# First input-projection unit by token blocks, next six units as three rounded products

## The reference

```
proj = h @ w_in                       # (256, 1024) @ (1024, 3328)
q_a, k_a, v_a, q_h, i_h, zf_fwd, zf_bwd, z_g = split(proj)
mix = concat(attention(q_a, k_a, v_a), recurrence(q_h, i_h, zf_fwd, zf_bwd, z_g)) @ w_out
h = layer_norm(alpha * h + mix)
for e in range(32): out += gate[:, e] * (swiglu(h @ w_up[e] + b_up[e]) @ w_down[e] + b_down[e])
h = layer_norm(alpha * h + out)
```

## Time and profile before

| | us |
|---|---|
| median of 3 runs | 1110.83 |
| the profiled execution, device time | 1110.73 |
| its span in the trace | 1109.0 |
| PE busy | 1043.1 (94% of the span) |
| DVE busy | 236.9 (21%) |
| ACT busy | 174.2 (16%) |
| HBM traffic | 428.31 MB, 386 GB/s mean |
| line L1040, records of 256 columns x272 | 62.0 busy, 391 ns for one |

### The profile page before, as it was taken

The page is one execution under the profiler, slowest core; times in us unless marked ns, Lnnn a source line. Parts: engine busy times, 40 slices in busy tenths (PEclk is TensorE's granted clock), DMA queues, the critical chain, the costliest instruction groups (busy, mean ns, idle before and its releaser), DMA issues.

```text
span 1109.0 us, 12478 instructions
## 1 busy us (share of the span) xinstructions
PE 1043.1 (94%) x5087; PEld 446.1 (40%) x5087; DVE 236.9 (21%) x650; ACT 174.2 (16%) x353; POOL 23.7 (2%) x31
## 2 busy tenths in 40 slices
PE   7999999999999999999999999999999999999995
PEld 6888656333333333333333333333333333333333
DVE  5186344111111111111111111111111111110114
ACT  2173211111111111111111111111111111110111
POOL 2500000000000000000000000000000000000000
PEclk8999999999999999999999999999999999999998
DMA  9733797999999999999999999999999999999993
GB/s 322 210 101 76 286 367 312 390 419 430 428 427 427 428 428 427 427 430 427 428 427 428 428 427 427 429 426 428 428 427 428 428 426 429 426 428 428 428 427 136
DMA packets 45934, 428.31 MB, mean 386 GB/s; under 512 B 4992, under 2 KB 18336, under 8 KB 21216
## 3 DMA queue, kind: packets, MB, share of 16 engines
q1 hardware_dynamic: 44352, 427.18, 92.9%
q10 hardware_dynamic: 1536, 0.43, 0.2%
HBM read 426.02 MB, written 1.05 MB: 385 GB/s over the span
## 4 chain that ended last, share of the span: by engine, by line
PE 67%; DMA 23%; DVE 7%; issue 2%; ACT 0%; DVEq 0%; ACTq 0%
PE bank L1291 27%; PE bank L1347 16%; DMA ring<-in_w_up_dram 15%; PE bank L1040 8%; PE bank L1246 4%; DMA lncat<-in_w_up_dram 4%; DMA mixa<-in_w_up_dram 4%; PE bank L1071 3%; DVE wbuf L971 2%; PE bank L1332 2%; DVE wbuf L966 2%; PE bank L1254 2%; DVE wbuf L975 1%; DVE wbuf L965 1%; PE bank L1302 1%
## 5 line engine op out<-in xcount | busy, mean ns | idle before, releaser
L1291 PE MATMUL bank<-ring,wbuf 128*64 128x512 f32 x1280 | 285.4, 593 | 9.4 <-DMA ring<-in_w_up_dram 9.4
L1291 PEld LDWEIGHTS bank<-ring,wbuf 128*64 128x64 f32 x1280 | 90.4, 137 | 187.3 <-issue 162.0
L1347 PE MATMUL bank<-ring,wbuf 128*64 128x512 f32 x640 | 145.0, 595 | 0.0
L594 ACT ACTIVATE wbuf<-wbuf 128x256 f32<-128x256 f32 x64 | 26.6, 416 | 480.3 <-DVE wbuf L965 480.3
L956 DVE TENSOR_SCALAR hT<-iota_s,hT 128x64 f32<-128x64 f32 x62 | 12.9, 251 | 409.1 <-PE bank L1291 409.1
L965 DVE TENSOR_SCALAR wbuf<-bank 128x256 f32<-128x256 f32 x64 | 26.9, 420 | 338.2 <-PE bank L1291 338.2
L1291 PE MATMUL bank<-wbuf 128*64 128x512 f32 x384 | 88.7, 593 | 0.4 <-DMA wbuf<-in_w_up_dram 0.4
L1347 PEld LDWEIGHTS bank<-ring,wbuf 128*64 128x64 f32 x640 | 44.6, 137 | 82.0 <-issue 79.6
L1261 PE MATMUL bank<-wbuf,putT 64*128 64x512 f32 x264 | 65.6, 615 | 0.7 <-ACT wbuf L604 0.7
L1040 PE MATMUL bank<-hT,wbuf 128*128 128x256 f32 x272 | 62.0, 391 | 2.4 <-ACT hT L464 2.4
L1246 PE MATMUL bank<-X,hT 128*64 128x512 f32 x256 | 62.0, 605 | 0.1
(11 more groups left out here) (240 smaller groups left out, 740.7 us busy)
## 6 DMA issues: line engine op xcount, KB each, us to landing
ring<-in_w_up_dram SPq DMA_DIRECT2D x80, 2048.0 KB, 31.4
ring<-in_w_down_dram SPq DMA_DIRECT2D x40, 2048.0 KB, 31.2
wbuf<-in_w_up_dram SPq DMA_DIRECT2D x24, 2048.0 KB, 31.1
mixa<-in_w_up_dram SPq DMA_DIRECT2D x12, 2048.0 KB, 32.9
lncat<-in_w_up_dram SPq DMA_DIRECT2D x12, 2048.0 KB, 32.2
wbuf<-in_w_down_dram SPq DMA_DIRECT2D x12, 2048.0 KB, 33.0
wbuf<-in_w_in_dram SPq DMA_DIRECT2D x13, 1024.0 KB, 9.8
mixa<-in_w_down_dram SPq DMA_DIRECT2D x6, 2048.0 KB, 33.2
```

What stands on the lines that cost most here:

```text
L594: a.activation(sig[:, w], glu[:, w], ACT.Sigmoid, scale=SIG_ALPHA).then_inc(s["sig_ready"], 1)
L1291: ins = mm(bank[n][c * SLOTS:(c + 1) * SLOTS, :], xT[:, k, :], wk[:, o:o + 512], start=(k == 0), stop=(k == KT - 1))
L1347: ins = mm(bank[2][c * SLOTS:(c + 1) * SLOTS, :], actT[:, at:at + SLOTS], wk[:, a * D + c * 512:a * D + (c + 1) * 512], start=(i == 0 and ...
```

## The change

Two things are changed in the input projection.

Unit 0 is worked by token blocks: for each token tile its 16 matmuls have 128 moving columns in place of 256, and each waits only for the parts of `hT` that it reads. The small transpose of `rows` is moved ahead of the first hT step on PE, and the copies of `embT` and `lbt` on DVE are moved to stand between the two token tiles.

Units 1 to 6 are each computed as three products of rounded operands. ACT writes a copy of the unit in float32r (`w_high`, 128 x 2048) and of hT (`h_high`, two copies of 128 x 1024). DVE subtracts them from the originals to get the low parts (`w_low`, written over the unit itself, and `h_low`). PE then adds up w_high x h_high, w_low x h_high and w_high x h_low, each over all eight k, in place of one float32 product. The high parts of the units go round four slots of `ring` (halves 6 to 9), `h_high` and `h_low` are in halves 10 and 11. The product w_low x h_low is left out.

The copies and subtractions are put between the other work of ACT and DVE as the diff shows: ACT makes the high parts of units 1 to 4 before the Exp table, its four DMA issues and `lb_exp`, and those of 5 and 6 after the copies of qa. DVE makes the low parts of units 1 and 2 and of hT before the small tensors, 3 after the wait for `lb_exp`, 4 after the work on X, and 5 and 6 between the copies of kv and `gates`.

```diff
@@ -4,6 +4,7 @@
 from concourse import mybir
 
 F32 = mybir.dt.float32
+F32R = mybir.dt.float32r
 BF16 = mybir.dt.bfloat16
 I32 = mybir.dt.int32
 U32 = mybir.dt.uint32
@@ -70,6 +71,7 @@
     UNITS = [(n, h) for n, _, w in GROUPS for h in range(w // 256)]
     UI = {u: i for i, u in enumerate(UNITS)}
     WBUF = 6
+    SPLIT = range(1, 7)
 
     with ExitStack() as ctx:
         def sb(name, shape, dt=F32):
@@ -82,6 +84,9 @@
 
 
 
+        with nc.sbuf_tensor("ring_r", [P, CHUNKS, CW], F32R) as ring_r, \
+                nc.sbuf_tensor("wbuf_r", [P, WBUF // 2, 4096], F32R) as wbuf_r:
+            pass
         ring = sb("ring", [P, CHUNKS, CW])
         halves = ring[:, :, :].rearrange("p c (a n) -> p (c a) n", a=2)
         wbuf = sb("wbuf", [P, WBUF // 2, 4096])
@@ -132,6 +137,15 @@
 
         def w_raw(u):
             return wbuf[:, u % WBUF // 2, u % 2 * 2048:(u % 2 + 1) * 2048]
+
+        halves_r = ring_r[:, :, :].rearrange("p c (a n) -> p (c a) n", a=2)
+        h_high, h_low = (halves_r[:, i, :].rearrange("p (k n) -> p k n", k=KT) for i in (10, 11))
+
+        def w_high(u):
+            return halves_r[:, 6 + (u - SPLIT[0]) % 4, :]
+
+        def w_low(u):
+            return wbuf_r[:, u % WBUF // 2, u % 2 * 2048:(u % 2 + 1) * 2048]
 
         lncat = sb("lncat", [P, 2 * TT * D])
         lnp = lncat[:, 0:2 * D].rearrange("p (i n) -> p i n", i=2)
@@ -205,7 +219,7 @@
         names = ("x_in0 x_in1 emb_in rows_in ln1_in ln2_in par_in "
                  "wout_in bias_in braw_in bup_split bup_in zeroed consts h_ready lb_ps proj_done job_done logf_ready logf_in exps_in "
                  "k_ready var_ready std_ready zg_sig mx_ready prob_ready prob_shared rec_cat rms_std mix_half "
-                 "mix_done hT_params x1_ready logit_done top_ready g4_ready mask_ready gate_ready "
+                 "mix_done hT_params h_high_ready h_low_ready w_high_ready w_low_ready x1_ready logit_done top_ready g4_ready mask_ready gate_ready "
                  "rank_done ex_ready route_done key_ready sel_ready plan_ps plan_ready lbm_ready lb_exp "
                  "kpT_ready aT_ready S_ready chunk_used picked put_ps gath_done xg_ready xT_ps actT_ps "
                  "scat_done plan_read put_ready xT_ready actT_ready y_ready glu_ready sig_ready act_ready "
@@ -468,6 +482,21 @@
                     if k == 2:
                         settle()
                 read(ins, ("hT", t, 0))
+
+            def high(u):
+
+                act.wait_ge(win_in[u % WBUF], 16 * (u // WBUF + 1))
+                if u - 4 in SPLIT:
+                    act.wait_ge(s["proj_done"], u - 4 + 1)
+                a.copy(w_high(u), w_raw(u)).then_inc(s["w_high_ready"], 1)
+
+            high(1)
+            for i in range(2):
+                for t in range(TT):
+                    job_is_read(act, ("hT", t, i))
+                a.copy(h_high[:, 4 * i:4 * i + 4, :], hT[:, 4 * i:4 * i + 4, :]).then_inc(s["h_high_ready"], 1)
+            for u in SPLIT[1:4]:
+                high(u)
             preload(ACT.Exp)
             act.dma_start(sink[:, :], attn_sink[0].partition_broadcast(P)).then_inc(s["par_in"], 16)
             act.dma_start(normg[:, :], hgrn_norm_g[0].partition_broadcast(P)).then_inc(s["par_in"], 16)
@@ -531,6 +560,8 @@
             q4 = qaT.rearrange("p j n -> p (j n)")
             tick(a.copy(tiles_of(q4, 0), pair("qa", 0)))
             a.copy(tiles_of(q4, 1), pair("qa", 1)).then_inc(proj_read[GI["qa"]], 1)
+            for u in SPLIT[4:]:
+                high(u)
             sig_gate(0)
             log_gate(0)
             probs(0)
@@ -642,9 +673,10 @@
                 link(v.reciprocal(rstd[:, t:t + 1], rstd[:, t:t + 1]))
                 v.tensor_scalar(X[:, t, :], X[:, t, :], mv[:, t, 0:1], rstd[:, t:t + 1], ALU.subtract,
                                 ALU.mult).then_inc(s["h_ready"], 1)
-            dve.wait_ge(s["lb_ps"], 1)
-            v.tensor_copy(embT[:, :, :], bank[7][:, 16:32].rearrange("p (m k) -> p m k", m=2)).then_inc(s["hT_params"], 1)
-            tick(v.tensor_copy(lbt[:, :, :, :], bank[7][:, 0:16].rearrange("p (d i h) -> p d i h", d=2, i=2)))
+                if t == 0:
+                    dve.wait_ge(s["lb_ps"], 1)
+                    v.tensor_copy(embT[:, :, :], bank[7][:, 16:32].rearrange("p (m k) -> p m k", m=2)).then_inc(s["hT_params"], 1)
+                    tick(v.tensor_copy(lbt[:, :, :, :], bank[7][:, 0:16].rearrange("p (d i h) -> p d i h", d=2, i=2)))
             dve.wait_ge(s["hT_params"], 1)
             for t in range(TT):
                 job_is_done(dve, ("hT", t, 1))
@@ -657,6 +689,20 @@
                         settle()
                 read(ins, ("hT", t, 1))
 
+            def low(u):
+
+                dve.wait_ge(s["w_high_ready"], u - SPLIT[0] + 1)
+                v.tensor_tensor(w_low(u), w_raw(u), w_high(u).bitcast(F32), ALU.subtract).then_inc(s["w_low_ready"], 1)
+
+            low(1)
+            for i in range(2):
+                dve.wait_ge(s["h_high_ready"], i + 1)
+                for t in range(TT):
+                    job_is_read(dve, ("hT", t, i))
+                k4 = slice(4 * i, 4 * i + 4)
+                v.tensor_tensor(h_low[:, k4, :], hT[:, k4, :], h_high[:, k4, :].bitcast(F32),
+                                ALU.subtract).then_inc(s["h_low_ready"], 1)
+            low(2)
             link(v.tensor_tensor(lbs[:, :, :], lbt[:, :, 0, :], lbt[:, :, 1, :], ALU.max))
             v.tensor_tensor(lbe[:, :, :, :], lbt[:, :, :, :],
                             lbs[:, :, :].unsqueeze(2).broadcast_to([P, 2, 2, NH]), ALU.subtract).then_inc(s["lbm_ready"], 1)
@@ -672,11 +718,13 @@
             link(v.tensor_tensor(lb[:, :, :], lbe[:, :, 0, :], lbs[:, :, :], ALU.mult))
             link(v.tensor_scalar(oml[:, :, :], lb[:, :, :], -1.0, 1.0, ALU.mult, ALU.add))
 
+            low(3)
             job_is_done(dve, ("hT", 1, 1))
             dve.wait_ge(s["emb_in"], 32)
             for t in range(TT):
                 link(v.tensor_tensor(X[:, t, :], X[:, t, :], lnp[:, 0, :], ALU.mult))
                 link(v.tensor_tensor(X[:, t, :], X[:, t, :], lnp[:, 1, :], ALU.add))
+            low(4)
             unit_is_done(dve, "kv")
             for g in range(NG):
                 for o in range(2):
@@ -684,6 +732,8 @@
             tick(v.tensor_copy(va[:, :, :], proj_bank("kv", 1)[:, 0:TOK].rearrange("p (t n) -> p t n", t=TT)))
             settle()
             dve.sem_inc(proj_read[GI["kv"]], 1)
+            low(5)
+            low(6)
 
             def cseq(ap):
                 return ap.rearrange("p (c n) -> p c n", n=HG_CHUNK)
@@ -1035,15 +1085,41 @@
                 def products(outs, columns=True):
 
                     for k in range(KT):
+                        if u == 0 and k % 4 == 0:
+                            for t in range(TT):
+                                if outs[0][2] == slice(t * P, (t + 1) * P):
+                                    job_is_read(pe, ("hT", t, k // 4))
                         for out, wc, hc in outs:
                             ops = (w[:, k, wc], hT[:, k, hc])
                             ins = mm(out, *(ops if columns else ops[::-1]), start=(k == 0), stop=(k == KT - 1))
                     return ins
 
+                def rounded(outs, columns=True):
+
+                    high, low = (x.rearrange("p (k n) -> p k n", k=KT) for x in (w_high(u), w_low(u)))
+                    for i, (wp, hp) in enumerate(((high, h_high), (low, h_high), (high, h_low))):
+                        if i == 0:
+                            pe.wait_ge(s["w_high_ready"], u - SPLIT[0] + 1)
+                            pe.wait_ge(s["h_high_ready"], 2)
+                        elif i == 1:
+                            pe.wait_ge(s["w_low_ready"], u - SPLIT[0] + 1)
+                        else:
+                            pe.wait_ge(s["h_low_ready"], 2)
+                        for k in range(KT):
+                            for out, wc, hc in outs:
+                                ops = (wp[:, k, wc], hp[:, k, hc])
+                                ins = mm(out, *(ops if columns else ops[::-1]), start=(i == 0 and k == 0),
+                                         stop=(i == 2 and k == KT - 1))
+                    return ins
+
+                if u in SPLIT:
+                    products = rounded
                 tiles = [slice(i * P, (i + 1) * P) for i in range(2)]
                 side_by = slice(half * 256, half * 256 + 256)
-                if name in ("zf0", "zf1", "qh", "qa"):
-
+                if u == 0:
+                    for t in range(TT):
+                        ins = products([(proj_bank(name, c)[:, tiles[t]], tiles[c], tiles[t]) for c in range(2)])
+                elif name in ("zf0", "zf1", "qh", "qa"):
                     ins = products([(proj_bank(name, c)[:, side_by], tiles[c], slice(0, TOK)) for c in range(2)])
                 elif name == "kv":
                     products([(proj_bank(name, 0)[:, 0:TOK], tiles[0], slice(0, TOK))])
```

(6 more changed lines are left out.)

## The result

| | before | after |
|---|---|---|
| median, beside each other | 1110.99 us (4 runs) | 1117.94 us (4 runs, 1117.12 to 1118.94) |
| ratio | 1 | 1.0068, interval 1.0055 to 1.0081 |
| the profiled execution | 1110.73 | 1118.94 |
| its span | 1109.0 | 1117.2 |
| granted clock, mean | 0.992 | 0.988 |

What follows compares the result with a forecast made beforehand. It took the front (PE's projections, DVE and ACT close behind) plus a fixed DMA weight stream as the bound. PE's gain of 9.8 us, cut by DVE to 7.4 at pT 0, gave 1110.7 - 7.4 = 1103.3 us; range 1100.5 to 1108.5.

Steps and rivals of the forecast that it cites:

- What bounds the kernel: Whole kernel: the end is the first pass plus a fixed weight stream; time won in the front reaches it one for one.
- The late DMA wait: Expert phase: it ends with the stream of weights; the chain's last DMA piece is 41.34 us long.
- The step that failed: DVE after its wait for `lb_exp` (31.2 us): small work, low 3, four X passes, then low 4 done at 41.5.
- The forecast wait of 2.4 before pT 0: End of the front: PE, ready at 57.5, waits 2.4 us for DVE's `shared` 0, which ends at 59.85.
- The price of a rounded record: PE, units 1 to 6: 109 ns a record, a unit 5.25 us in place of 7.0; kv's values also 5.25.
- The rival of slow records: PE, units 1 to 6: rounded records at the float32 rate, 18.8 us slower, 1129.5 us; decides from 148 ns; chance 0.14.
- ACT and DVE alone: Copies and subtractions: 2048 columns cost 1.9 us on ACT, 2.3 on DVE, adding 13.5 and 16.3 us.
- Unit 0: PE's first projection unit: starts at 11.9 us in place of 14.02, ends at 21.1 against 23.4.
- changes it by nothing: Clock during PE's first unit: no effect on the end, since unit 4's landing, ACT, `lb_exp` and DVE set the time.
- The vector chain eats it: DVE before `gates`: later unit 4 or longer subtractions cost 4 us more; gain 0 to 3, about 1109 us; chance 0.09.
- PE stalled behind low 3 or low 4 for over 1 us: PE at units 3 and 4: a listed sign that the forecast is wrong; the forecast itself had a wait of 0.3 us.

Runs made afterwards that it cites:

- the split left out: Changed kernel without POOL's six operations splitting b_up into bfloat16 parts (experts' up bias missing from the result): 1104.00 us, ratio 0.9940.
- X set under it: Kernel before, with DVE's four passes over X waiting until b_up is in, so they run while POOL splits it: 1108.61 us, one run.
- kv in float32: Changed kernel with POOL's b_up split later, DVE's work earlier, unit 2 unrounded and ACT's qa copies ahead of the table load: 1100.03 us, ratio 0.9902.
- unit 0 alone: Changed kernel without rounded units: only token blocks and the moved small transpose and copies: 1104.72 us, ratio 0.9942; again 1106.76 us, ratio 0.9957.
- the split after `S_ready`: Changed kernel with POOL's b_up split held until DVE ends both directions, SP's copy of it behind the w_out loads: 1103.58 us, ratio 0.9946.

## Why the prediction was wrong, and where it was right

**What bounds the kernel.** Right. Once the clock's 1.5 us is taken out, the end moves with the front one for one, to 0.5 us in each row of the table. The late DMA wait stays, only later: its piece of the chain starts at 1017.03 in place of 1009.05.

**The step that failed.** "Behind that wait stand 0.8 of small work, low 3 (34.3), four passes over X (4.9, to 39.2), low 4 (41.5)". It priced six operations at 9.5 us by rows that had run beside no POOL; they took 23.5. It named DVE's idle time as the cover and did not ask who else worked in it: from 34.97 to 50.99 POOL did. The change moved the passes over X from 19.03 to 37.06, because the later `lb_exp` and low 3 stand before them. The runs with the split left out and with X set under it show cause and price.

From there the numbers close. PE starts on low 4 at 56.78 in place of 41.5, 15.3 later: 1.1 of it by `lb_exp`, 14.0 by POOL, the rest small work. It had stood idle for 13.57 us and its clock fell, as these stretches of after show (columns as above):

```profile
55.00:60.00 5.00, 3.22 (x15) 0.50 0.00 0
60.00:64.00 4.00, 4.00 (x25) 0.69 0.00 0
```

At 1.2 GHz for the most part, the 32 records took 6.60 us, against 3.5 in the sum: 3.1 more (2.8 by the clock, as 32 such records take 3.84 at full rate, 0.3 by their price). The last two units took 11.71 against 10.5, 1.2 more. The forecast wait of 2.4 before pT 0 fell away. 15.3 + 3.1 + 1.2 - 2.4 = 17.2, and pT 0 is 77.02 against 59.85.

**The price of a rounded record.** A size was off, the mechanism right. At 256 columns 32 records take 4.00 us less 0.16 for the tail, 120 ns each, where 109 was taken. At 128 columns, for the values of kv, 24 records lie between the starts of 30.57 and 33.24, 111 ns each. These are rows of after:

```profile
30.57 1.06 PE L1111 MATMUL bank<-wbuf_r,ring_r 128*128 128x128 f32 x8
31.46 1.95 PE L1111 MATMUL bank<-ring_r 128*128 128x128 f32 x16
...
33.24 1.06 PE L1111 MATMUL bank<-wbuf_r,ring_r 128*128 128x128 f32 x8
...
39.21 4.00 PE L1111 MATMUL bank<-ring_r 128*128 128x256 f32 x32
```

Half the columns take 9 ns off 120, so the stream is not what bounds the record. A load of weights near the 106 ns that the sum worked out fits both prices; no run separates it from another cost that each record has. A unit is 5.76 us (7.0 before), and kv is 24 x 120 + 48 x 111 ns = 8.2 (7.0 before): rounding loses 1.2 us there, which the prediction did see in part and which the run with kv in float32 gives back. The expectation of that run had 119 ns and 8.6 us, read from a row that holds 16 records of 256 columns beside 8 of 128. The rival of slow records (148 ns and more) is out, and with it the rule of the Trainium skill that was weighed ("TensorE: Matmul & The Clock Gate", Part 3): load plus stream would be 213 ns.

**ACT and DVE alone.** Right. 1.89 to 1.91 us for a high part (1.9) and 2.29 for a low part that meets nobody (2.3). With the split left out the next step of the forecast came as well: PE waited before pT 0 for DVE's `shared`, 0.59 us where 2.4 was forecast, and pT 0 started at 61.13, 1.3 behind the sum.

**Unit 0.** The end of unit 0 was near (20.97 against 21.1) by luck: it started 1.3 later than forecast (13.22; 11.83 in the run of unit 0 alone), and the clock was back sooner. The claim that the clock in unit 0 "changes it by nothing" held where unit 4's landing, ACT and DVE set the time: in the runs with the split left out and with the split after `S_ready` the clock from 12 to 20 us was 1.00 and 0.83, and pT 1 starts at 77.51 and 77.44. It does not hold with that chain out of the way: at pT 0 unit 0 alone is worth 4.6 us with the clock kept, 2.2 in the run where it had fallen before the transposes.

**The rivals.** The slower side was given to slow records alone, decided on PE. "The vector chain eats it" had the right place, DVE before `gates` and low 4, and among its reasons that "DVE's subtractions of two tensors run longer", but it was priced at 4 us, with a floor at no loss, and by no row; the price was 14.0, and it put PE's stall on the path. The sign "PE stalled behind low 3 or low 4 for over 1 us" was the one that came true.

## What to carry to other kernels

Before work is put into an engine's idle time, look at what the other engines do in that stretch: it may be what keeps the work of both at its own length. Price every DVE operation with two inputs in SBUF that can meet a POOL operation by the length of that operation, down to the ones on 8 columns; `gates`, with one tensor in SBUF, was held up too, while operations with an input in PSUM and a reduction were not. Place POOL's work where DVE has slack. Three rounded products for one of float32 paid here at 256 columns a record (5.76 us against 7.0) and lost at 128 (5.3 against 3.5), since a rounded record costs nearly the same at both widths.

## What the runs showed of the hardware that was not expected

- An operation of DVE on 128x8 elements took 3.92 us in place of 0.17, and POOL's took up to 6.03 in place of 4.07: when both have work of the kinds above, they go in turns, one whole operation each.
- Rounded records cost 120 ns at 256 columns and 111 at 128, where the float32 records, two to a product, cost 218 and 109: the narrower tile costs the rounded type nearly as much.
- Undoing half of the change made it faster (1115.24 against 1117.94). In the traces about half of the 3.1 us at low 4 goes with a change of order between two engines half a microsecond apart, the other half with an earlier `lb_exp`.
- The clock in the stretch from 150 to 200 us is full in some runs and 0.97 in others of nearly the same kernel. Of the kernel before's runs beside the experiments, seven of the eight with a mean clock of 0.995 lie from 1108.2 to 1109.2 us, and all but one of those with 0.992 or 0.993 from 1110.3 to 1112.4. What decides it was not tried.
